# Run-wise alternation of the streamed columns in the split dense products

## The reference

```python
rq, rk, rv, rg, mq, mk, mv, mo, mg, gr, gm = _split_in(_modulate(x, norm1_g, sh1, sc1) @ w_in)
crq, crk, crv, ... = _split_in(_modulate(ctx, norm1_g, csh1, csc1) @ w_in)
merged = sigmoid(g_r) * (yr @ w_ret_out) + sigmoid(g_m) * (ym @ w_mlstm_out)
x = x + gt1 * (merged @ w_out)
x = x + gt2 * _peer(_modulate(x, norm2_g, sh2, sc2), peer_query, peer_keys, peer_down, peer_up)
...
proj = rms_norm(x, g_pre[l]) @ w_in[l]                  # second block, input projection
merged = gates[:, :, 0] * (y_a @ w_br_pool[l]) + ...    # second block, four branches
x = x + rms_norm(merged @ w_out[l], g_post[l])
```

## Time and profile before

| | us |
|---|---|
| timed runs: median (lowest to highest) | 3402.79 (3399.61 to 3404.13) |
| the profiled execution: span from first to last instruction | 3398.1 |
| opening, up to 407 | 407 |
| first block, 407 to 930 | 523 |
| peer stage, 930 to 2266 | 1336 |
| second projection, 2266 to 2811 | 545 |
| second merge, 2811 to the end | 587 |

### The profile page before, as it was taken

One profiled execution on the slowest core, in us unless ns is written; L12 is line 12 of the kernel. 1 busy time (PEld: TensorE's weight loads), 2 busy tenths in 40 slices (PEclk: granted clock), 3 DMA queues, 4 the chain that ended last, 5 costly groups with the idle time before them and its releaser, 6 DMA issues. The chain is left out here.

```text
span 3398.1 us, 30787 instructions
## 1 busy us (share of the span) xinstructions
PE 2891.6 (85%) x11248; PEld 2039.2 (60%) x11248; DVE 1824.5 (54%) x2377; ACT 1145.6 (34%) x1860; POOL 2339.1 (69%) x1120
## 2 busy tenths in 40 slices
PE   6999999999986666655656766589999999999998
PEld 2787888888753333322222322248888888888887
DVE  3577537412678777778988887751147412111122
ACT  3322356544421111111221112134455444444443
POOL 0244677588667575756776577858767698888887
PEclk9999999999988888877788887789999999999999
DMA  9999855365699999999999999985545456656554
GB/s 401 334 344 337 308 171 171 126 230 195 242 420 424 425 426 426 426 427 427 417 427 427 427 427 427 427 322 188 171 154 187 139 196 194 227 190 206 191 191 163
DMA packets 308075, 1015.86 MB, mean 299 GB/s; under 512 B 21932, under 2 KB 26640, under 8 KB 241104
## 3 DMA queue, kind: packets, MB, share of 16 engines
q1 hardware_dynamic: 231336, 475.62, 40.4%
q0 software_dynamic: 73728, 536.90, 37.5%
q10 hardware_dynamic: 2860, 1.38, 0.1%
HBM read 1009.59 MB, written 4.24 MB: 298 GB/s over the span
## 5 line engine op out<-in xcount | busy, mean ns | idle before, releaser
L729 POOL TENSOR_TENSOR block_weights_lo<-weight_ring,block_weights_hi 128x1024 fp32r<-128x1024 f32 x596 | 1445.0, 2433 | 575.2 <-ACT block_weights_hi L722 560.7
L1911 PE MATMUL banks<-up_rows,pick_diagonal 128*128 128x512 f32 x1024 | 673.1, 819 | 446.5 <-DMA up_rows<-peer_up,picked_experts 385.9
L722 ACT ACTIVATE block_weights_hi<-weight_ring 128x1024 fp32r<-128x1024 f32 x608 | 640.9, 1059 | 997.2 <-PE banks L3065 315.3
L1911 PEld LDWEIGHTS banks<-up_rows,pick_diagonal 128*128 128x128 f32 x1024 | 260.3, 267 | 827.2 <-issue 736.0
L1768 POOL DMA_INDIRECT up_rows<-peer_up,picked_experts x256 | 480.2, 1876 | 335.4 <-PE banks L1911 111.4
L2274 DVE CUSTOM_DVE_ANT_0 down_rows<-down_rows,h_tokens 128x2048 f32<-128x2048 f32 x256 | 583.8, 2291 | 183.1 <-DMA down_rows<-peer_down,picked_experts 177.2
L1760 POOL DMA_INDIRECT down_rows<-peer_down,picked_experts x256 | 408.0, 1594 | 105.6 <-issue 76.8
L2221 DVE SCALAR_TENSOR_TENSOR expert_sum<-up_rows,pick_share,expert_sum 128x2048 f32<-128x2048 f32 x125 | 293.9, 2351 | 51.4 <-ACT pick_share L2055 45.6
L2049 ACT ACTIVATE pick_gelu<-pick_dots 128x2 f32<-128x2 f32 x127 | 25.7, 203 | 837.7 <-DVE pick_dots L2274 837.5
L2499 PE MATMUL banks<-block_weights_hi,h_T_hi 128*128 128x512 f32 x688 | 272.8, 396 | 2.3 <-POOL block_weights_lo L729 2.3
L2501 PE MATMUL banks<-block_weights_hi,h_T_lo 128*128 128x512 f32 x688 | 268.3, 390 | 0.0
(11 more groups left out here) (549 smaller groups left out, 4339.0 us busy)
## 6 DMA issues: line engine op xcount, KB each, us to landing
weight_ring<-w_in SPq DMA_DIRECT2D x232, 1024.0 KB, 5.0
cond_ring<-w_ada SPq DMA_DIRECT2D x128, 512.0 KB
weight_ring<-w_ada SPq DMA_DIRECT2D x32, 1024.0 KB, 8.1
weight_ring<-w_out SPq DMA_DIRECT2D x32, 1024.0 KB, 4.9
weight_ring<-peer_query SPq DMA_DIRECT2D x12, 1024.0 KB, 16.4
weight_ring<-w_ret_out SPq DMA_DIRECT2D x8, 1024.0 KB, 4.9
weight_ring<-w_mlstm_out SPq DMA_DIRECT2D x8, 1024.0 KB, 4.9
weight_ring<-w_mem_kv SPq DMA_DIRECT2D x8, 1024.0 KB, 11.3
```

What stands on the lines that cost most here:

```text
L722: act.activation(self.hi[:, self.place(slot, h)], ring.tile[:, slot, h * self.HALF:(h + 1) * self.HALF], ACT.Copy).then_inc(self.hi_ready, 1)
L729: pool.tensor_tensor(self.lo[:, at], ring.tile[:, slot, h * self.HALF:(h + 1) * self.HALF], self.hi[:, at], ALU.subtract).then_inc(ring.us ...
L1911: mm = pe.matmul(ps[:, 4 + b], diag[:, G % 2], up[:, p % ROWS, b * CG:(b + 1) * CG], start=(G % PER_TB == 0), stop=(G % PER_TB == PER_TB - ...
```

## The change

A helper `alternating(ap, ways, run)` is added. It takes the 512 columns of an operand as `ways` equal parts and walks them in runs of `run` columns, one run from each part in turn. It is applied to the streamed weights and to the output bank alike, so that each weight column still meets its own sum. With (2, 16) the columns go 0 to 15, 256 to 271, 16 to 31, 272 to 287, and so on; with (2, 32) in runs of 32; with (4, 16) the runs come from columns 0, 128, 256 and 384. A column is 4 bytes, so the parts lie 1 KiB apart, or 512 bytes with four. The opening gets (2, 16), the first block (2, 32), the second projection (4, 16). The second merge and the sixteen triples in the peer stage stay as they are. No instruction is added, removed or moved on any engine, and no wait is changed.

```diff
+def alternating(ap, ways, run):
+
+    return ap.rearrange("p (r i j) -> p i r j", r=ways, j=run)
...
@@ phase_opening
-                    (hi, lo), w_hi, w_lo = lhs(k, j), split.hi[:, at, kk], split.lo[:, at, kk]
-                    pe.matmul(out_bank(q), hi, w_hi, start=(k == 0), stop=False, skip_group_check=True)
-                    pe.matmul(out_bank(q), hi, w_lo, start=False, stop=False, skip_group_check=True)
-                    mm = pe.matmul(out_bank(q), lo, w_hi, start=False, stop=(k == KB - 1), skip_group_check=True)
+                    hi, lo = lhs(k, j)
+                    out, w_hi, w_lo = (alternating(ap, 2, 16) for ap in (out_bank(q), split.hi[:, at, kk], split.lo[:, at, kk]))
+                    pe.matmul(out, hi, w_hi, start=(k == 0), stop=False, skip_group_check=True)
+                    pe.matmul(out, hi, w_lo, start=False, stop=False, skip_group_check=True)
+                    mm = pe.matmul(out, lo, w_hi, start=False, stop=(k == KB - 1), skip_group_check=True)
@@ phase_first_block
-                        out, w_hi, w_lo = ps[:, 2 * (g % 2) + tb], split.hi[:, at, kk], split.lo[:, at, kk]
+                        out, w_hi, w_lo = (alternating(ap, 2, 32) for ap in (ps[:, 2 * (g % 2) + tb], split.hi[:, at, kk], split.lo[:, at, kk]))
@@ phase_second_projection
-                            out, w_hi, w_lo = ps[:, 2 * (c % 2) + tb], split.hi[:, at, kk], split.lo[:, at, kk]
+                            out, w_hi, w_lo = (alternating(ap, 4, 16) for ap in (ps[:, 2 * (c % 2) + tb], split.hi[:, at, kk], split.lo[:, at, kk]))
```

## The result

| | before | after |
|---|---|---|
| median of the timed runs | 3401.84 us | 3441.99 us (3441.24 to 3446.14) |
| ratio | | 1.0122, 95% interval 1.0110 to 1.0134 |
| span of the profiled execution | 3398.1 us | 3439.9 us |
| opening, first start to first start of the next stage | 341.4 us | 356.6 us |
| first block, to the first gathered matmul | 542.1 us | 556.7 us |

The change makes the kernel slower by 1.2%: the prediction was wrong in sign, and the time lies 7 us above its range. The four longer stages give 15.2 + 14.6 + 1.1 + 11.0 = 41.9 us, and the spans differ by 41.8 us. The borders here are exact starts, so the lengths differ from those of the rounded windows ahead of the prediction.

The account below looks back on a forecast made before the run. PE's matmul pace was taken to bound the three changed stages. Savings of 22.1 (second projection) + 10.1 (first block) + 8 (opening) - 1 (POOL) = 39 us gave 3364 us; the 8-in-10 range was 3346 to 3435.

Parts of the forecast that it names:

- What bounds the kernel: Opening, first block, second projection: nobody keeps PE waiting, so time is number of matmuls times pace, 0.227 us per 512 columns.
- What a jump between runs may save: Three changed stages: 10.7 ns saved per matmul with runs of 16, half with runs of 32; 22.1, 10.1 and 8 us.
- The weight load has no part in it: Dense stages: gate matmuls load 32 or 16 stationary columns, dense ones 128, yet 256 columns take half the pace, 0.1133 us.
- That a stream can collide is seen elsewhere: Second merge: one stretch runs at 0.233 us per matmul with same instruction and clock, taken as collision with something in memory.
- The float32 row as the best case: Dense matmuls: at best the float32 pace without its lost cycles, 213.3 + 3 = 216 ns, 10.7 ns less than now.
- The opening's discount: Opening: 14.4 us of gain cut to 8 us, because the DMA engines are at 0.95 there.
- POOL's price of 1 us: POOL delivers half tiles to a faster PE: covered by 0.12 us or more, yet 1 us of the gain given back.
- no cost of issue, wait or DMA: Whole change: no instruction is added or moved, so nothing is charged for these.
- The second story: Changed stages: the lost cycle belongs to each 64 bytes wherever they lie; pace stays 0.2267 us, 3403 us; chance 0.30.
- The third rival: Changed stages: each jump costs a cycle, on weights or bank of sums; 3461 us, 3432 if half pay; chance 0.25.
- The last line of the signs: Profile after: different paces for (2, 16) and (4, 16) would mean the parts' distance matters, which no case costs.

Follow-up runs that it names:

- m1_patterns: Kernel of its own, only matmuls, 33 in a row per column order, against reading in order: (2, 16) takes 240.0 ns, in order 226.7.
- m2_operands: Matmul-only kernel varying stationary columns, their place, streamed columns and orders: one stationary column 228.9 ns in order; stationary start moved 4 to 64 columns, 227.0 to 233.4.
- all_32_4: Against the kernel before: order (32, 4) in the opening, first block, second projection and second merge; 3382.66 us, ratio 0.9946.
- m3_pitches: Matmul-only kernel varying the length and pitch of the column pieces read: pieces of 16 columns take 226.7 ns at pitch 40, 242.1 at pitch 64.
- start_24_in_order: Against the kernel before: weight tiles of the opening and first block start 24 columns (96 bytes) further on, read in order; 3417.51 us, ratio 1.0048.

## Why the prediction was wrong

**What bounds the kernel: right.** In the stages that the change touches, PE waits for nobody and the time is the number of matmuls times their pace. After, 1344 x 11.8 + 1896 x 9.2 + 2064 x 6.0 ns give 15.9 + 17.4 + 12.3 = 45.6 us; the three stages grew by 40.8. Of the 4.8 us between, 2.3 are idle time of PE, which fell from 14.7 to 12.4 us over the three stages by the exact borders; the rest is in the matmuls whose distance to the next start is not in the mean, and was not taken apart.

**The failing step is "What a jump between runs may save".** It took 10.7 ns per matmul as saved, because the loss of 32 cycles has the period of the run, 64 bytes, so that it had to come where one piece follows its neighbour. Nothing was saved: measured is a loss of 13.3 ns more with (2, 16), 10.0 more with (2, 32) and 4.4 to 10.0 more with (4, 16). The period was a coincidence of numbers: 17/16 is what reading in order gives from a start at 0; from a start 8 columns on the same stream loses 48 cycles, from one column repeated it loses 6. Nor is a neighbour needed for a loss: the same 16 columns read over lose 69. What the runs show in its place is that the loss goes with the series of places, mostly within 64 columns, that the stream visits. (2, 16) and (4, 16) come back to the same place after each run; of the runs of 128 and more, those that go on at the right place keep the pace of reading in order. (32, 4) goes from one 64-byte piece to the next after each 16 bytes and gains. That the series is the cause is shown by changing it alone (order, start, pitch); by what mechanism it costs is not.

**"The weight load has no part in it": half right.** Without it the loss stays (228.9 ns with one stationary column), but where the stationary columns lie moves the pace by up to 6.8 ns. I took the gate columns' half pace for a proof; it was one that could not see a place. It does not even hold with 128 stationary columns: 256 streamed columns then take 120.0 ns (m1_patterns), and 113.6 with one of them repeated.

**"That a stream can collide is seen elsewhere": the reading pointed the wrong way.** A pace of 0.233 with the same instruction is what places a few columns off give in the small kernels. It showed that the pace depends on places, and so that 0.2267 is a good case that a new order could lose; I used it only for the gain. The row names what is different in that stretch: the stationary operand is `p_split`, a tile at another place. Over the whole merge of before, the matmuls that load it have a mean of 231.5 ns and those that load `h_T_hi` 227.0; in the opening and the first block `lat_split` stands at 230.7. That fits the stationary start of m2_operands (up to 233.4), but no run moved `p_split` itself.

**The float32 row as the best case: right as a bound, wrong as a value.** 429 ns, 6 lost cycles, stands in all orders. The records there are halves: m1_patterns shows that a float32 matmul leaves two of them, so the seven were not seven matmuls, and a float32 matmul takes 858 ns, 3.8 times the 226.7 of float32r and not about twice, as the description of the kernel has it. With two cycles for each column in each record it says nothing of an order at one. The best that any order with float32r gave is 220.0 ns alone and 224.9 in the kernel.

**The opening's discount was not put to the test.** I let the loads hold back a gain, and there was none; the DMA share fell from 0.95 to 0.90. Where there was a gain, in all_32_4, the opening kept 3.1 of 4.3 us and PE waited 1.6 us for loads: the right side, on a small scale.

**POOL's price of 1 us and "no cost of issue, wait or DMA": right.** POOL's mean is 2421 ns against 2423, and PE's wait for it in the second projection 1.7 us against 2.3.

**The second story failed with the forecast.** It had the pace stay at 0.2267 in any order of aligned 64-byte pieces; no stage stayed there.

**The third rival was the right side, with another mechanism, so its numbers were in part luck.** It foretold 0.240 for runs of 16 and 0.233 for runs of 32. It met the opening (0.240) exactly, and missed the first block (0.237) and the second projection (0.231 to 0.237). A cycle a run gave 58 us; 41.8 came, chiefly because (4, 16) pays for a third of its runs through most of the stage. The bank of sums, named in it, pays nothing. I gave it 0.25 and let the range end where half of its jumps pay; the witness for cheap jumps was L515, one jump of 8 KiB. By m3_pitches jumps of 2 and of 4 KiB that go on at the next place within 256 bytes are free; if that holds for 8 KiB, L515 could not have shown a cost.

**The last line of the signs was the useful one.** "A pace that differs between (2, 16) and (4, 16) would say that the distance of the parts matters, which none of my cases costs": it differs, 0.240 against 0.231.

**Open** is the rule itself: which series of places loses how many cycles, and how the stationary columns' place comes into it. Open is also why (4, 16) goes from 0.232 us in the mean to 0.237 from about 2720 us on in the second projection, with the same line and order; it is the same end of the stage in which (32, 4) gains nothing.

## What to carry to other kernels

A surplus over the number of columns in a float32r matmul's pace is a matter of places: of the order of the streamed columns, of their start, and of the stationary columns' start. Measure such an order alone, as 33 matmuls in a row and by the distance of their starts, before a kernel is built on it; here that gave the pace of (2, 16) and (2, 32) to 0.2 ns and that of (4, 16) to about 1 ns for most of its stage, though (32, 4) gained only part of what it gained alone, and the one start that I transferred with it missed by 6 to 8 ns. An engine without waits has no cover, so each nanosecond of its pace counts almost in full, in either direction, and a period that fits a number is not a mechanism.

## What the hardware showed that I had not expected

- A float32r stream of 512 columns takes between 220.0 ns (528 cycles; 215.8 with one column repeated) and 461.3 ns, by its order and its start alone; bfloat16 takes 215.8 in order, in (2, 16) and in (2, 32), and 226.8 in (2, 4); float32 takes 429.2 a record in all three orders tried.
- Fewer columns do not scale: 384 take 173.5 ns (416 cycles, 32 lost, as with 512), 256 take 120.0 or 113.6, 448 take 206.7.
- Moving the split weight tiles of two stages by 96 bytes costs a whole kernel 0.5%, with not one instruction changed (start_24_in_order).
- Writing the bank of sums in runs of 16 and 32 columns costs nothing that the kernel shows, 0.9999 (0.9989 to 1.0009).
- 128 runs of 16 bytes each are faster than one run of 2 KiB, 223.4 against 226.7 ns alone and 224.9 against 228.1 in the kernel's merge.
